# The second stream's tokens moved behind the first stream's in the entry stage, and work reordered around four waits of the convolution layer

## The reference, cut to what matters

```python
h = rmsnorm(x) * (1 + scale) + shift       # for x, and likewise for ctx
u, gate = split(h @ w_in)                  # the mixer's inputs and its gate
...
x = x + gate_x * rmsnorm(mix(u, gate) @ w_out)
```

## Time and profile before

| What | Value |
|---|---|
| median of three runs | 1930.19 us |
| lowest, highest | 1928.72, 1931.47 us |
| the profiled execution's own time | 1932.57 us |
| its span, first to last instruction | 1930.7 us |
| mean granted TensorE clock, as a share of full | 0.987 |
| TensorE busy | 1856.5 us (96%) |
| VectorE, ScalarE, GpSimd busy | 812.1, 404.1, 60.1 us |
| DMA | 367.82 MB, mean 191 GB/s |

### The profile page before, as it was taken

How to read it: one execution, slowest core, us unless ns; L and a number is a source line. 1 busy time by engine, 2 the same in 40 slices (tenths; PEclk the granted TensorE clock), 3 DMA queues, 4 the chain that set the end, 5 groups by cost and what they waited for, 6 DMA issues and landing times.

```text
span 1930.7 us, 17977 instructions
## 1 busy us (share of the span) xinstructions
PE 1856.5 (96%) x6829; PEld 968.8 (50%) x6829; DVE 812.1 (42%) x2046; ACT 404.1 (21%) x994; POOL 60.1 (3%) x78
## 2 busy tenths in 40 slices
PE   6999999999999999999999999999998999999997
PEld 2545564444555544443344855588855434444432
DVE  3874545863855666425655234353332100100101
ACT  2121332001852122201113214211101111111111
POOL 0000000000000000004410000000000000000000
PEclk9999999999999999999999999999998999999999
DMA  9654101452102343410203330434394999999994
GB/s 405 234 213 175 44 1 55 184 208 102 52 1 99 123 162 122 153 66 22 71 1 141 112 123 18 174 123 167 107 388 183 428 428 427 426 428 427 428 428 173
DMA packets 31398, 367.82 MB, mean 191 GB/s; under 512 B 3676, under 2 KB 3789, under 8 KB 6349
## 3 DMA queue, kind: packets, MB, share of 16 engines
q1 hardware_dynamic: 31308, 366.62, 47.8%
HBM read 365.52 MB, written 1.09 MB: 190 GB/s over the span
## 4 chain that ended last, share of the span: by engine, by line
PE 92%; DVE 4%; ACT 1%; POOL 1%; issue 1%; DMA 1%; SPq 0%; DVEq 0%; ACTq 0%; POOLq 0%
PE bank L793 14%; PE bank L2767 11%; PE bank L695 9%; PE bank L1796 8%; PE bank L2804 6%; PE bank L1632 4%; PE bank L1349 3%; PE bank L2754 3%; PE bank L1161 3%; PE bank L2788 3%; PE bank L876 3%; PE bank L2201 2%; PE bank L1477 2%; PE bank L1989 2%; PE bank L898 2%; PE bank L1515 1%
## 5 line engine op out<-in xcount | busy, mean ns | idle before, releaser
L793 PE MATMUL bank<-hT,slot 128*128 128x256 f32 (+1 forms) x832 | 268.0, 480 | 0.4 <-DVE open_o L816 0.4
L793 PEld LDWEIGHTS bank<-hT,slot 128*128 128x128 f32 x832 | 157.3, 191 | 99.4 <-issue 87.1
L407 DVE SCALAR_TENSOR_TENSOR product<-slot,cond_rows 128x1024 f32<-128x1024 f32 x160 | 195.6, 1223 | 8.7 <-DVE product L407 2.8
L1796 PE MATMUL bank<-hT,slot 128*128 128x512 f32 (+1 forms) x416 | 171.4, 567 | 1.7 <-DVE hT L738 1.7
L695 PE MATMUL bank<-slot,gT 128*128 128x512 f32 x384 | 167.0, 594 | 0.0
L2841 DVE SCALAR_TENSOR_TENSOR hT<-hT,bank 128x512 f32<-128x512 f32 x16 | 11.0, 688 | 261.0 <-ACT hT L2873 261.0
L1796 PEld LDWEIGHTS bank<-hT,slot 128*128 128x128 f32 x416 | 78.9, 194 | 77.8 <-issue 73.7
L695 PEld LDWEIGHTS bank<-slot,gT 128*128 128x128 f32 x384 | 72.7, 191 | 88.4 <-issue 88.2
L2804 PE MATMUL bank<-slot,hT 128*64 128x512 f32 x256 | 92.1, 595 | 0.0
L2767 PE MATMUL bank<-slot,scratch 128*64 128x512 f32 x256 | 90.6, 592 | 1.2 <-ACT scratch L2865 1.2
L1632 PE MATMUL bank<-slot,hT 128*128 128x512 f32 x192 | 82.7, 592 | 0.0
(11 more groups left out here) (395 smaller groups left out, 2619.2 us busy)
## 6 DMA issues: line engine op xcount, KB each, us to landing
slot<-panels_dram SPq DMA_DIRECT2D x91, 2048.0 KB, 9.6
late_slots<-panels_dram SPq DMA_DIRECT2D x40, 2048.0 KB, 20.4
slot<-panels_dram SPq DMA_DIRECT2D x40, 1024.0 KB, 5.2
branch_slot<-panels_dram SPq DMA_DIRECT2D x9, 2048.0 KB, 23.2
mod_slot<-panels_dram SPq DMA_DIRECT2D x4, 2048.0 KB, 17.4
slot<-panels_dram SPq DMA_DIRECT2D x4, 1536.0 KB, 7.2
gate_rows_all<-gate_rows_dram SPq DMA_DIRECT2D x4, 1024.0 KB, 8.7
slot<-panels_dram SPq DMA_DIRECT2D x2, 1280.0 KB, 17.7
```

What stands on the lines that cost most here:

```text
L407: last = m.nc.vector.scalar_tensor_tensor(out=m.product[:], in0=m.slot(panel)[:, c * D:(c + 1) * D], scalar=1.0, in1=m.cond_rows[:, s, :], ...
L793: last = self.m.nc.tensor.matmul(self.bank(g), self.m.slot(panel)[:, k * width + j * P:k * width + (j + 1) * P], self.m.hT[:, k, 0:self.n] ...
L1796: last = nc.tensor.matmul(ps[g % 2][:, tokens], m.slot(i)[:, k * 512 + g % 4 * P:k * 512 + (g % 4 + 1) * P], m.hT[:, k, tokens], start=k = ...
```

## The change

In the entry stage the token tiles of the context are loaded behind the second modulation panel and `a_cq0`, and squared, normed, transposed and scaled behind those of `x`, while TensorE does the first two latents. In the convolution layer four groups of channels instead of two begin before the context's tiles are there (the last tile's transposes stand ahead of the fourth); the first gate group stands ahead of the last group's transposes; the first round's filter is made and paired before and beside the last gate group; `inverse` waits matmul by matmul, with the odd part first; and the transposes of the second half of the result are left to the next stage, which runs them after its first four matmuls. The other operations are the same.

```diff
@@ enter_first
+            load_tokens(STREAMS[0])
             m.issue(sp, panels[CHUNKS[0]])
...
             m.issue(sp, m.index("a_cq0"))
+            load_tokens(STREAMS[1])
             m.issue(sp, panels[CHUNKS[2]])
             m.issue(sp, panels[CHUNKS[3]])
@@ tensor
             product(0)
-            for t in range(NT):
+            for t in STREAMS[0]:
                 turn_tokens(t)
             product(1)
...
             first_half_of_latents(0)
+            first_half_of_latents(1)
+            for t in STREAMS[1]:
+                turn_tokens(t)
+            pe.wait_ge(by_act.sem, by_act.at(NX + 1))
             product(2)
-            first_half_of_latents(1)
+            first_half_of_latents(2)
+            pe.wait_ge(by_act.sem, by_act.at(NT))
+            product(3)
+            pe.wait_ge(by_dve.sem, by_dve.at(NT))
             turn_columns(2)
-            product(3)
-            first_half_of_latents(2)
             turn_columns(3)
             first_half_of_latents(3)
@@ vector (ScalarE's loop has the same form)
+            for s, stream in enumerate(STREAMS):
+                norm = slice(NORM + NX * s, NORM + NX * (s + 1))
+                dve.wait_ge(squares.sem, squares.at(NX * (s + 1)))
+                inverse_root(m, dve, m.sums[:, norm], 1.0 / D, m.var[:, norm], m.rstd[:, norm], m.tmp[:, norm])
+                for t in stream:
...
+                if s == 0:
+                    take_chunk(0)
+                for t in stream:
+                    take_turned(t)
+                if s == 0:
+                    take_chunk(1)
+                    take_columns(0)
+                    take_columns(1)
+                    dve.wait_ge(modulation.sem, modulation.at(1))
...
+            take_chunk(2)
+            take_chunk(3)
+            take_columns(2)
+            take_columns(3)
@@ enter_layer, tensor
+            half_first = m.late_turn is not None
             for t in range(NT):
-                m.tile_of_gT(pe, t)
+                if t == 0 and half_first:
+                    pe.wait_ge(m.gT_half_ready[0].sem, m.gT_half_ready[1])
+                else:
+                    m.tile_of_gT(pe, t)
...
+                        if half_first and (t, n, k) == (0, 0, KD // 2):
+                            m.last_tile(pe)
+                            m.tile_of_gT(pe, 0)
@@ conv_inputs, tensor
-            for g in range(2):
+            for g in range(AHEAD):
+                if g == AHEAD - 1:
+                    m.last_tile(pe)
                 channels(g, slice(0, N))
-            m.last_tile(pe)
             m.tile_of_hT(pe, NT - 1)
             for g in range(CH + 1):
...
+                else:
+                    pe.wait_ge(filter_units.reduced.sem, filter_units.reduced.at(2))
+                    pe.wait_ge(*m.loaded(panels[6]))
+                    gates.matmuls(pe, 0, panels[6], 0)
...
-            for g in range(8):
+            for g in range(1, 8):
...
+                if g == 7:
+                    pe.wait_ge(paired.sem, paired.at(2))
+                    pe.wait_ge(filter_units.sines.sem, filter_units.sines.at(2))
+                    pe.wait_ge(read.sem, read.at(CH - KD))
+                    pe.wait_ge(*m.loaded(filters.w3))
+                    for t in range(NX):
+                        filters.products(pe, 0, t, ROUNDS[0])
                 gates.matmuls(pe, g, i, g % 4)
@@ conv_inputs, vector
             for g in range(8):
                 gates.doubled_silu(dve, g, m.gT[:, g, :])
-                if g == 5:
+                if g == 6:
+                    dve.wait_ge(*m.loaded(filters.decay))
+                    for t in range(NX):
+                        filters.pair(dve, 0, t, ROUNDS[0])
+                if g == 4:
...
@@ conv_rounds, tensor
             def inverse(r, s):
-                pe.wait_ge(combined.sem, combined.at(2 * PER * r + PER * (s + 1)))
-                for part, fs in enumerate(((0, 3), (2, 1))):
-                    for f in fs:
...
+                for i, (f, _, _, _) in enumerate(recipe):
+                    part = 0 if f in (0, 3) else 1
+                    pe.wait_ge(combined.sem, combined.at(2 * PER * r + PER * s + i + 1))
+                    last = nc.tensor.matmul(ps[2 * s + part][:, :], idft[:, f, :], prod[:, s, f, :], start=i < 2, stop=i >= 2)
+                    if i >= 2:
+                        last.then_inc(back.sem, back.one())
...
-            pe.wait_ge(*m.loaded(filters.w3))
-            filters.products(pe, 0, *rounds[0])
-            m.earlier(pe, m.sig("gate_done"))
-            filters.products(pe, 1, *rounds[0])
...
+                    if r == 0 and g == 3:
+                        m.earlier(pe, m.sig("gate_done"))
...
-            turn(1)
+            m.late_turn = lambda pe: turn(pe, 1)
@@ conv_rounds, scalar (the odd part is copied when it is done; VectorE waits for both)
-                    act.wait_ge(back.sem, back.at(4 * r + 2 * s + 2))
+                    act.wait_ge(back.sem, back.at(4 * r + 2 * s + 1))
```

More of the change, by code:

```diff
@@ L429, in enter_first @@
     panels = m.take(4, *[f"mod0.{n}" for n in range(4)])
-    norm = slice(NORM, NORM + NT)
-    CHUNKS = (0, 2, 1, 3)
+    CHUNKS, STREAMS = (0, 2, 1, 3), (range(0, NX), range(NX, NT))
     token_bank = lambda t, half: ps[4 + 2 * (t % 2) + half]
@@ L1753, in sine, with conv_inputs @@
         self.m.nc.scalar.activation(self.h[i][:], self.h[i][:], ACT.Sin).then_inc(self.sines.sem, self.sines.one())
-def conv_inputs(m, u, filter_units, w3, columns):
+ROUNDS = [(order, half) for order in range(2) for half in range(2)]
+def conv_inputs(m, u, filter_units, filters, columns):
     nc, ps = m.nc, m.ps
@@ L1795, in channels @@
                 for k in range(KD):
-                    last = nc.tensor.matmul(ps[g % 2][:, tokens], m.slot(i)[:, k * 512 + g % 4 * P:k * 512 + (g % 4 + 1) * P],
+                    last = nc.tensor.matmul(bank(g)[:, tokens], m.slot(i)[:, k * 512 + g % 4 * P:k * 512 + (g % 4 + 1) * P],
                                             m.hT[:, k, tokens], start=k == 0, stop=k == KD - 1)
@@ L1906, in __init__, with bank, products @@
         self.both = m.cond_rows[:].rearrange("p t (w c) -> p t w c", w=2)
-        self.banks = (2, 6)
         self.ready, self.made = m.sig("filter_in_psum"), m.sig("filter_pair_ready")
-    def products(self, pe, t, order, half):
+        self.ready_at, self.made_at = self.ready.total, self.made.total
+    def bank(self, r, t, way):
+        return self.m.ps[((2, 0) if r == 0 else (2, 6))[t] + way]
+    def products(self, pe, r, t, what):
+        order, half = what
         for way in range(2):
@@ L1913, in products, with pair @@
             at = order * D + half * 512
-            last = self.m.nc.tensor.matmul(self.m.ps[self.banks[t] + way][:, :], self.h2[rows, t * P:(t + 1) * P],
+            last = self.m.nc.tensor.matmul(self.bank(r, t, way)[:, :], self.h2[rows, t * P:(t + 1) * P],
                                            self.m.slot(self.w3)[rows, at:at + 512], start=True, stop=True)
         last.then_inc(self.ready.sem, self.ready.one())
-    def pair(self, dve, r, t, order, half):
+    def pair(self, dve, r, t, what):
+        order, half = what
         v, both, cols = self.m.nc.vector, self.both, slice(half * 512, (half + 1) * 512)
-        dve.wait_ge(self.ready.sem, self.ready.at(NX * r + t + 1))
+        dve.wait_ge(self.ready.sem, self.ready_at + NX * r + t + 1)
         for way in range(2):
-            last = v.tensor_tensor(both[:, t, way, :], self.m.ps[self.banks[t] + way][:, :], self.fall[:, t, cols], ALU.mult)
+            last = v.tensor_tensor(both[:, t, way, :], self.bank(r, t, way)[:, :], self.fall[:, t, cols], ALU.mult)
         if t == 0:
@@ L1935, in conv_rounds @@
     nc, ps = m.nc, m.ps
-    rounds = [(order, half) for order in range(2) for half in range(2)]
+    rounds = ROUNDS
     R = len(rounds)
@@ L2038, in gate @@
                                                    op0=ALU.mult, op1=ALU.mult).then_inc(turned_read.sem, turned_read.one())
-            m.earlier(dve, m.sig("gate_done"))
-            dve.wait_ge(*m.loaded(filters.decay))
-            for t in range(NX):
-                filters.pair(dve, 0, t, *rounds[0])
             for r, (order, half) in enumerate(rounds):
```

128 lines of the change are left out of this document (58 added, 70 removed).

## The result

The changed kernel took 1913.72 us, the median of four runs (1911.38 to 1914.88), beside 1929.86 us for the kernel before in four runs of its own: a ratio of 0.9914, with an interval of 0.9897 to 0.9931. That is 16.1 us less; the forecast was 1908.6 us, 21.6 under the 1930.19 it started from, with a range of 1904.5 to 1916.0 that holds the result. The profiled execution took 1913.51 us, with a span of 1911.7 us and a mean granted clock of 0.989, beside 1930.7 us and 0.987 before: 19.0 us less from span to span.

The account below looks back on a forecast made before the run. TensorE, busy 1856.5 of 1930.7 us, bounds the kernel, so only its pauses and half-clock work can be won back. Gains of 2.0, 6.6, 8.9 and 4.1 make 21.6 us: 1908.6 us against the median, range 1904.5 to 1916.

Parts of the forecast that it names:

- Entry stage: Start of the kernel: panel 0 comes 2.5 us earlier, less 0.4 us for the column turns; gain 2.0 us.
- upper bound of 4.2: Entry stage: gain of 4.2 us if the half clock of the first latent goes too.
- Entry of the convolution layer: Up to channel group 4: no pause or half clock left but one 0.85 us wait for VectorE; gain 6.6 us.
- Channels to first spectrum: Channels' end to first spectrum's end: taps and pairing covered by gate groups, 75.4 us becomes 66.5; gain 8.9 us.
- Rounds: Convolution rounds: no gain, since the next spectrum waits for the second pairing, whose place in VectorE's order is the same.
- End of the rounds: Last inverse to projection: four projection matmuls stand in the pause, and the projection runs at full clock; gain 4.1 us.
- Sum: Whole kernel: the stage gains 2.0, 6.6, 8.9 and 4.1 add up to 21.6 us.
- so they shift as a whole: Later stages: triggered by TensorE's own progress, they move earlier unchanged, so the 21.6 us are kept.
- margin for the clock: Pauses left in the changed stages: clock falls of 1.7 us each, once or twice; the range reaches 1916.
- the profile was carried over to the median: Whole kernel: profiled execution 2.4 us above the median, so 1911.0 us profiled would be 1908.6 against the median.
- the clock falls in pauses that are left: First latent, 0.85 us wait, last round: half clock costs 1.7 us once or twice; 1911 us, chance 0.15.
- The rival at 1913, the filter not ready: Behind gate group 7: filter late, the 4.6 us gap ahead of the spectrum stays; 1913 us, chance 0.09.
- the experts' stage at 428 GB/s: Experts' slices: the stage goes at DMA's pace and the gain is given back; 1930 us, chance 0.03.

Follow-up runs that it names:

- turn_undone: The changed kernel with the last transposes of the result back in the rounds' stage, the projection behind them: 1913.47 us, ratio 0.9910.
- before_filled: The kernel before with 18 idle products of constants in pauses of the second half's entry and the router: 1925.99 us, ratio 0.9978.
- after_again: The changed kernel run again without any edit, five executions, beside the kernel before: 1908.65 us, ratio 0.9891.
- the filled kernels: The kernels before and after with 18 idle products each (1925.99 and 1906.43 us), and the latter with ten more (1904.05 us).

## Why the prediction was right, and what it missed

- **Entry stage, 2.0 us.** The stage gained 1.9 in the first pair of profiles and the panel 2.9 instead of 2.5; the next pair gave 0.5, and the average over all profiles is 1.7, so the close hit of the first pair is in part luck. The upper bound of 4.2 should be 3.9 by its own terms (2.0 + 5.37 - 3.43); `turn_undone`, without half clock there, reached 49.11 - 45.09 = 4.0. The tiles and panels landed in the order of their issue in the profiles of both kernels; what the Trainium skill, DMA: Bandwidth & Descriptors, section Queues, rings and completion order, says, that completion is not first in, first out, did not show in this queue.
- **Entry of the convolution layer, 6.6 us.** 6.3 measured. The one wait left, put at 0.85 us, was 0.80. That VectorE's queue and not TensorE's would hold TensorE once, by 0.85 us, is the step that the trace bears out.
- **Channels to first spectrum, 8.9 us.** 75.4 to 66.5, 8.9. `c_w3` was issued at 824.7, landed at 832.5, and its products began at 845.3, so there were 12.8 us between them, 13.0 in the working.
- **Rounds, 0.** The kernel is 16.9 us ahead at the spectrum of each of the three later rounds, so the rounds themselves gave nothing.
- **End of the rounds, 4.1 us.** 4.1 measured, but the working put it to the late turn. Undone alone it is worth 2.0; the odd part first (0.7 us) and the clock (0.9 + 0.6 us) make the rest. The clock's part isn't the edit's: in `before_filled` it stayed up behind the full pause of 2.47 us.
- **Sum, 21.6 us.** 21.0 us at 991.57 us of the kernel after, 19.5 in the second pair, where the entry stage gave less.
- **What the forecast missed.** 1908.6 us was 5.1 too low, though inside the range. 0.6 of that are the stages. 2.0 are the step "so they shift as a whole": the later stages shift, but the clock's stretches in them don't stay as they are. In both pairs of profiles 1.7 us were given back at 1209 and 0.4 from 1424 us on, in untouched code, behind pauses that are as long as before. The forecast's margin for the clock looked at the pauses of the four stages alone. The last 2.4 to 2.5 are in how the profile was carried over to the median: the forecast took off 2.4 us because the profiled execution of the kernel before was so much above its median (1932.57 and 1930.19), but that of the changed kernel is at its median (1913.51 and 1913.72).
- By executions, the forecast is right for the three of nine at a mean clock of 0.992 (1908.0 to 1908.7 us) and 3 to 6 us too low for the six at 0.989 and 0.990 (1911.4 to 1915.0). The median of the first four is 1913.72, that of the other five 1908.65.
- The rival "the clock falls in pauses that are left", 1911, has the mechanism that did cost time, but at another place than it named. Of the pauses it named, the 0.80 us wait and the 1.9 us ahead of the first turn left the clock up, and the half clock at the first latent was there before the change too.
- The rival at 1913, the filter not ready, is nearest by number and refuted by the trace: there is no pause between gate group 7 and the spectrum. `c_w3` was in time, and the experts' stage at 428 GB/s gave back 0.2 to 0.3 us of TensorE's gain.

The Trainium skill, TensorE: Matmul & The Clock Gate, section What's actually happening, adds that the number of slow matmuls at the start of one kernel differs from run to run. The traces here agree for the start (half clock at the first latent in eight profiles of the new entry stage, none in `turn_undone`), and show it in the middle of a kernel too: 6.8 us at the window attention in the kernel after and 3.4 in `turn_undone`, which is the same program up to there.

## What to carry to other kernels

Where TensorE carries the chain, price a pause together with the clock behind it, and cover it with independent work of the same engine; ask then which queue (here VectorE's) becomes the slower one. When two edits cover one pause, undo each alone before giving either the whole gain. If gains in the stages and gain in time differ, multiply each execution's span with its mean granted clock: the difference that this takes away is at most the clock's. Then follow the distance between the two kernels from place to place, and hold the clock up with a few idle products in the pauses of untouched stages: what is still lost there is a cost of the change. Here nothing was. And take more than one profile: one stage gave 1.9 us in the first pair and 0.5 in the second.

## What the runs showed that was not expected

- One kernel has two groups of times, in `after_again` 6.5 us apart (1908.3 and 1914.9 us), which the mean granted clock, 0.992 and 0.989, tells apart. No profile fell on the lower group. `turn_undone` shows two places where the clock can stay up, 25 and 484 us, the filled kernels two more; which of them make the lower group isn't shown.
- Half clock can last far longer than the pause ahead of it: in the router, 17.1 us behind pauses of 0.84 and 2.31 us, with products of 36 columns between them. Timeline, kernel after:

```profile
1422.25 1.95 PE L2649 MATMUL bank<-vecs,hT 128*128 128x36 f32 x16 [0.84 <-ACT hT L1191]
1426.50 1.97 PE L1168 MATMUL bank<-cst,gate_rows_all 128*128 128x128 f32 x8 [2.31 <-DVE gate_rows_all L1270]
1429.31 3.60 PE L2649 MATMUL bank<-vecs,hT 128*128 128x36 f32 x16 [0.84 <-ACT hT L1191]
```

- 28 products of 256 columns that compute nothing made the kernel 7 to 9.5 us faster by mean span than the same kernel without them (1902.1 beside 1911.6 and 1909.1, on different chips), and its runs lie within 1.4 us of each other.
